# A ring of weight stages: four slots in place of seven

## The reference, cut to what matters

```
mod   = silu(c) @ w_ada + b_ada                    # adaLN shift, scale, gate: 2 layers x 6 x 1024
layer 0: h = rmsnorm(x) * (1 + sc) + sh
         proj = h @ a_w_in                         # q, k, v, o and gates of 8 heads
         mLSTM in both directions, group norm, sigmoid(o) * hs @ a_w_out
         SwiGLU: (silu(h @ w1a) * (h @ w1b)) @ ff_w2          # 3584 wide
layer 1: conv mixer: GLU(h @ b_w_pw1), depthwise conv of 31 taps, norm, silu, @ b_w_pw2
         top-2-of-8 experts, each a SwiGLU 3584 wide
out   = rmsnorm(x)
```

## Time and profile before

| | us |
|---|---|
| median of 3 runs (lowest, highest) | 1948.01 (1946.86, 1949.96) |
| the profiled execution's own time | 1949.14 |
| its span, first to last instruction | 1947.4 |
| TensorE busy in the span | 1799.9 (92%) |
| VectorE busy, ScalarE busy | 1414.6 (73%), 1029.6 (53%) |
| ring transfers: experts / mixers / dense SwiGLU | 252 of 1536 KB / 92 of 1024 KB / 28 of 1536 KB |
| their median time from issue to landing | 8.4 / 6.5 / 6.5 |
| HBM traffic over the span | 292 GB/s |
| mean granted TensorE clock, share of full | 0.960 |

### The profile page before, as it was taken

One profiled execution on the slowest core, in us unless ns is written; L12 is line 12 of the kernel. 1 busy time (PEld: TensorE's weight loads), 2 busy tenths in 40 slices (PEclk: granted clock), 3 DMA queues, 4 the chain that ended last, 5 costly groups with the idle time before them and its releaser, 6 DMA issues.

```text
span 1947.4 us, 24369 instructions
## 1 busy us (share of the span) xinstructions
PE 1799.9 (92%) x8764; PEld 1453.1 (75%) x8764; DVE 1414.6 (73%) x1602; ACT 1029.6 (53%) x975; POOL 48.3 (2%) x95
## 2 busy tenths in 40 slices
PE   5899998899999784779999999999999999999993
PEld 1788774489999562558888888888888888888883
DVE  1444341255655797369999999999999999999995
ACT  1222121143333102167777777777777777777772
POOL 0011000000000000000000000000000000000001
PEclk9999999999999886879999999999999999999997
DMA  9366568535553562379999999999999999999972
GB/s 387 117 232 225 211 217 329 194 115 180 192 191 122 224 263 103 135 289 378 378 376 377 380 382 377 376 376 386 369 387 376 376 382 374 378 377 378 385 298 86
DMA packets 62999, 568.53 MB, mean 292 GB/s; under 512 B 7268, under 2 KB 7396, under 8 KB 15204
## 3 DMA queue, kind: packets, MB, share of 16 engines
q1 hardware_dynamic: 54144, 539.13, 71.9%
q0 software_dynamic: 5392, 19.41, 2.7%
q10 hardware_dynamic: 3412, 9.28, 1.2%
HBM read 549.43 MB, written 18.36 MB: 292 GB/s over the span
## 4 chain that ended last, share of the span: by engine, by line
PE 82%; DVE 10%; DMA 3%; issue 2%; ACT 2%; POOL 0%; DVEq 0%; POOLq 0%; SPq 0%; ACTq 0%
PE ps L1448 21%; PE ps L1450 21%; PE ps L1449 21%; PE ps L1309 5%; DVE work L1096 5%; PE ps L1431 4%; PE ps L1306 3%; DMA ring<-mix 2%; PE ps L1582 1%; DVE w_lo L1206 1%; PE ps L1245 1%; ACT w_hi L782 1%; PE ps L1356 1%; PE ps L1416 1%; PE ps L1326 1%
## 5 line engine op out<-in xcount | busy, mean ns | idle before, releaser
L1206 DVE TENSOR_TENSOR w_lo<-ring,w_hi 128x1536 fp32r<-128x1536 f32 x504 | 873.5, 1755 | 76.5 <-ACT w_hi L782 76.1
L782 ACT ACTIVATE w_hi<-ring 128x1536 fp32r<-128x1536 f32 x504 | 750.8, 1492 | 232.2 <-PE ps L1450 221.9
L1448 PE MATMUL ps<-w_hi,hg 128*128 128x512 f32 x1008 | 398.3, 395 | 4.4 <-DVE w_lo L1206 4.4
L1450 PE MATMUL ps<-w_hi,hg 128*128 128x512 f32 x1008 | 393.6, 390 | 0.0
L1449 PE MATMUL ps<-w_lo,hg 128*128 128x512 f32 x1008 | 393.2, 390 | 0.0
L1448 PE MATMUL ps<-w_hi,hid 128*128 128x512 f32 x616 | 242.0, 393 | 3.0 <-DVE hid L1200 3.0
L1449 PE MATMUL ps<-w_lo,hid 128*128 128x512 f32 x616 | 240.1, 390 | 0.0
L1450 PE MATMUL ps<-w_hi,hid 128*128 128x512 f32 x616 | 239.9, 389 | 0.0
L1448 PEld LDWEIGHTS ps<-w_hi,hg 128*128 128x128 f32 x1008 | 189.9, 188 | 42.6 <-DVE w_lo L1206 4.8
L1450 PEld LDWEIGHTS ps<-w_hi,hg 128*128 128x128 f32 x1008 | 189.6, 188 | 40.1
L1449 PEld LDWEIGHTS ps<-w_lo,hg 128*128 128x128 f32 x1008 | 190.0, 189 | 38.0
(11 more groups left out here) (225 smaller groups left out, 1671.7 us busy)
## 6 DMA issues: line engine op xcount, KB each, us to landing
ring<-moe SPq DMA_DIRECT2D x252, 1536.0 KB, 8.4
ring<-mix SPq DMA_DIRECT2D x92, 1024.0 KB, 6.5
ring<-ff SPq DMA_DIRECT2D x28, 1536.0 KB, 6.5
xg<-work POOLq DMA_DIRECT2D x12, 512.0 KB, 4.7
so<-xg POOLq DMA_DIRECT2D x10, 512.0 KB, 8.4
yg<-so ACTq DMA_DIRECT2D x10, 512.0 KB, 9.5
work<-c POOLq DMA_DIRECT2D x8, 257.0 KB, 7.2
c_out<-work ACTq DMA_DIRECT2D x8, 257.0 KB, 5.8
```

Of the source, the lines that this page charges most:

```text
L782: act.activation(w_hi[:, s % W_BUFS, :], ring[:, sl, s % 2 * CUT * ROW:(s % 2 + 1) * CUT * ROW], ACT.Copy).then_inc(hi_ready, 1)
L1206: TT(w_lo[:, s % W_BUFS, :], ring[:, slot(ST_MOE + s // 2), s % 2 * CUT * ROW:(s % 2 + 1) * CUT * ROW], w_hi[:, s % W_BUFS, :].bitcast(f32 ...
L1448: pe.matmul(out, a_hi, b_hi, start=start, stop=False)
L1450: return pe.matmul(out, a_lo, b_hi, start=False, stop=stop)
```

## The change

SLOTS becomes 4. The ring then takes 48 KB of each partition in place of 84 KB; the slot of each stage, the number of semaphores, the number of transfers issued at the start, the unrolling of SyncE's loops and every wait of a transfer for a freed slot follow from that constant. No other work, operand, shape or order changes on any engine. The freed 36 KB are not used for anything.

```
-SLOTS = 7
+SLOTS = 4
```

## The result

| | before | four slots |
|---|---|---|
| median, us (6 runs each) | 1947.77 (1946.86 to 1950.65) | 1957.26 (1952.70 to 1959.39) |
| profiled execution's own time | 1949.14 | 1959.39 |
| its span | 1947.4 | 1957.7 |
| TensorE busy | 1799.9 | 1802.9 |

The medians are 9.5 us apart. The ratio is 1.0045, with a 95% interval of 1.0034 to 1.0056: between 6.6 and 10.9 us. The forecast was 1957.0 with a range of 1953.5 to 1963.5. The two profiled executions differ by 10.25 us.

A forecast was written before the change was run, and what follows sets the result against it. TensorE's matmuls were taken to set the time of the experts and dense SwiGLU. Refill +7.5 and clock +1.5 gave +9.0 us on 1948.0, so 1957.0 us, range 1953.5 to 1963.5.

The forecast's parts named there:

- Where it costs and where not: Whole kernel: 0 wherever landing time is below the room; the only cost is the adaLN stages of iterations 14 and 15.
- The refill of the burst: adaLN stages 46 to 55, iterations 14 and 15: stage 55 lands at 317.7, not 310.2, +7.5 us.
- The lower bound: Same adaLN stages: at today's quickest stretch, 2.4 us a stage, the added wait is +7.2 us.
- How the queue stays full: Stages 53, 54 and 55 are freed some 9 us or more before landing, so they follow at 2.5 us each.
- Iteration 15's own chain is ready when stage 55 is today: Iteration 15: heads, norm and transpose are ready by then, so nothing else covers the wait for stage 55.
- The clock: TensorE at 1.2 GHz behind the wait: 0.9 on stage 55 and 0.6 on `gate_rows`, +1.5 us in all.
- Sum: 7.5 + 1.5 = +9.0 us: 1958.1 against the profiled execution, 1957.0 for the median.
- The chain's DMA share: Ring wait near 300 us in the chain grows from 10.8 to about 18 us, beginning in iteration 14.
- Experts running dry: Experts' landings exceed their thin cover at some items: +9 us (1966) up to +50 (2007); chance 0.14, 0.04 far above.
- Refill speeding up: iterations 14 and 15: a shallower queue lands needed stages sooner; half the gain gives about +4 us; chance 0.07.
- no change: The 10.83 us wait near 300 us is set by something other than queued bytes, so nothing shows; chance 0.03.

The follow-up runs named there:

- the kernel at depth five: Seven-slot kernel before, with only SyncE's waits for stages 7 to 63 made as late as five slots would make them: 1953.68 us, ratio 1.0033.
- filler: Four slots plus TensorE matmuls of constants, results unused, ahead of each of stages 49 to 55: 1956.84 us (1.0039), repeated 1954.62 us (1.0040).
- the even spread: The mixer's 24 adaLN stages spread three per two iterations, not five each in 14 and 15: seven slots 1952.87 us (1.0021), four slots 1951.13 us (1.0013).
- depth three: Seven-slot kernel before, with only the experts' transfers made to wait as late as three slots would: 2046.73 us, ratio 1.0527.
- three tail stages in place of five: Three adaLN stages each in iterations 14 and 15, the other four moved earlier: four slots 1947.84 us (0.9994), seven slots 1943.39 us (0.9965).

## Why the prediction was right, step by step

- *Where it costs and where not.* Right, and shown by splitting the change: the mixer's waits alone have the loss, all waits from stage 64 on together 0.9997. In the experts landings stayed at 8.4 us, 9.7 at most. The dense SwiGLU's first split waited 20.8 us longer for its stage (41.6 for 20.8), as forecast from a transfer issued 20.7 us later, and that did not reach the chain. In pw1 TensorE waited 0.6 us for the ring once, which it did not do before; that is not on the chain either.
- *The refill of the burst, +7.5 (7.2 to 8.9).* From stage 46 to 55 it took 23.0 - 14.9 = 8.1 us more. Stage 50 was awaited at 304.15, as forecast ("near 304"), stage 55 at 318.71 for 317.7. The slope of about 2.5 us a slot is shown by the kernel at depth five. Landings are issue times plus times to landing: stage 53 at 301.4 + 10.8 = 312.2, stage 54 at 305.6 + 10.6 = 316.2, stage 55 at 318.6. The forecast had 312.7, 315.2 and 317.7, so the excess came between 53 and 54, 4.0 us apart where 2.5 were counted; what delayed stage 54 was not shown. The lower bound's 2.4 us a stage stands in no row either: the closest landings of before read here, of stages 55 and 57, are 5.0 us apart, 2.5 a stage.
- *How the queue stays full.* One statement was wrong in part: that 53, 54 and 55 are freed some 9 us or more ahead of their landings. Stage 55 was issued at 312.1, 6.5 us ahead. The reason is iteration 15's own work: its matmuls stand behind stage 50 in TensorE's order, so stage 50's lateness pushed them from 301 to 305, and stage 51 was used only at 310.88. The low clock lengthened them too (L1353 took 1.92 us for 1.03), which I had left out. Neither mattered, because stage 54 was still landing (awaited until 316.23): with filler they are short, stage 51 is used at 310.10, and stage 55 starts at 318.77 all the same.
- *"Iteration 15's own chain is ready when stage 55 is today."* Right. The head was normed at 308.11 and stage 55's matmuls began at 310.28; TensorE turned to the head at 311.28. I did not size this margin of 3.2 us. For four slots it decided nothing (normed at 314.03, stage 55 at 318.71). It bounds what the ring's wait costs the kernel before, of which 10.8 us were expected back from the even spread.
- *The clock, +1.5 (0 to 3.2).* It was 12.2 - 9.8 = 2.4: 0.9 on stage 55 and 0.7 on `gate_rows` (forecast 0.9 and 0.6), and 0.8 on `ada_turn` (1.86 for 1.04), which I had left out. The granted clock was 0.50 from 320 to 326 us and 1.00 from 330 to 336, so it was back when the projection began, as assumed. The filler kernel shortens just these pieces.
- *Sum.* +9.0 forecast; 8.1 + 2.4 = 10.5 in the profiled stretch, 9.5 between the medians. Both terms were a little small. That the median of 1957.26 lies 0.3 us from the forecast is in part luck; the profiled execution's own time, 1959.39, is 1.3 above the 1958.1 said for it.
- *The chain's DMA share.* I said that the wait near 300 us would grow from 10.8 to about 18 us in the chain. It reads 7.14 + 6.52 = 13.7: iteration 15's matmuls now stand on the chain between the two waits. Stage 55's own start is the better measure.
- *The rivals.* Experts running dry: did not happen, but at depth three it costs 96 us. Refill speeding up and no change: fell with stage 55's start. The Trainium skill (SBUF — State Buffer, "A bandwidth-pool intuition that's wrong") puts the path from HBM to a core at about 358 GB/s, half of a stack's 716. The experts moved 378 GB/s with four slots as well, so the measurement decides.

## What to carry to other kernels

A ring's depth is judged place by place: a slot's room is the time that its users spend on the other slots, and it has to exceed the landing time under load; where it does, further slots gave nothing here, and where it does not, the whole phase runs at about (landing + held) / depth, with both times as they are in that state. The exception is a burst that uses stages up faster than they can be fetched: there every slot is worth one transfer, once for the whole burst. With three tail stages in place of five, four slots are level with the old kernel, but only because a wait of 3.6 us elsewhere went with the new order. Before a burst is taken apart, look for the wait that it fills, and for the idle time where its stages go. The chain names only the wait that ends last, and its length is not what its removal gives: 10.83 us stood in the chain, and the next wait ended some 3 us before it.

## What the runs showed of the hardware

The landing time of the experts' transfers was 8.4 us at the median with seven, four and three slots allowed, at one transfer in 4.25, 4.25 and 4.63 us, and 6.5 us with two, at one in 6.08. So above two it did not depend on how many slots were allowed. In the first three about two transfers were under way on average (8.4 / 4.25 = 2.0), in the last about one (6.5 / 6.08 = 1.1); which of the pace and this overlap sets the landing time was not separated.

TensorE at its lower level of 1.2 GHz was seen on stage 55 in every profiled four-slot burst without filler (1.93 or 1.94 us in place of 1.07), and from 301.81 on in the burst at depth five. In the burst before, where stage 55 alone was waited for (1.68 us), it took 1.07. With 1.1 us of small matmuls ahead of each of the stages 49 to 55, stage 55 took 1.06 us, and the granted clock was 1.00 from 297 to 318.8.
